# Feed-forward up projections of a two-layer encoder step: eight block products per pair of units replaced by seven

## The chip, the cores and the metric

The kernel runs on one core of a Trainium2 chip. The metric is the device time of one execution in microseconds (us). Before the change the median of 3 runs is 1405.25 us (1405.14 to 1405.56).

## What is computed

One step of a hybrid encoder with 2 layers on 512 prompt tokens and 32 sample tokens, kept side by side as 544 columns; the model width is 1024 and everything is float32. Each layer does

```python
hn = rmsnorm(x)
# retention (4 heads), gated linear attention (4 heads) and band attention (8 heads) from hn @ w_in
x = x + concat([A, B, C]) @ w_out
u = rmsnorm(x) @ w_up                       # 1024 -> 4096
x = x + square(relu(u)) @ w_down            # 4096 -> 1024
```

and a last rmsnorm follows. The change lies in `u`, the up projection, and in what stands around it.

## The kernel before

Activations lie in SBUF as tiles of 128 features by T = 544 tokens; KC = 8 such tiles make the width. A *unit* is a block of 1024 inputs by 128 outputs of a weight matrix, one [128, 1024] tile. A layer has 28 units of input projections, 8 of the output projection (`N_IN + m`) and, in GROUPS = 4 groups, 8 up units and 8 down units each (`N_MLP = 16` a group). So 100 units a layer.

A float32 product is made from two parts of each factor in the type float32r: a *high* part (a copy rounded by ACT) and a *low* part (DVE: the value less its high part). A unit's weights arrive in one of four buffers `raw` (SP, `load`, line 322, which waits until the unit four before it has its low part); ACT writes `whi` (`split`, line 495), DVE `wlo` (`rest`, line 840), in two slots each. PE then runs `products` (line 1376): for each of 8 input tiles high x high, high x low and low x high, each for two halves of HT = 272 tokens, so 48 matmuls of 128x128 weights by 272 columns into two banks of PSUM. Units use two banks of four in turn. Line 1366 records nearly all matmuls.

The feed-forward part: the last output unit's residual is added by DVE (line 1227), ACT makes the scaled high part `xhi` (line 469), DVE the low part `xlo` (line 817), ACT a square that POOL sums up (line 439) for the second norm; POOL then reduces over the partitions (line 445). The norm's factor is applied only to the down projection's result: it is a positive number per token, so it passes through relu and the square as a square, `r2` (lines 1273 and 1278, made once for each group). An up unit's result goes through ACT (relu into `nt`, line 712), DVE (times itself, line 1248), ACT (high part `zhi`, line 715) and DVE (low part `zlo`, line 1251). The down unit 0 waits for these one by one (`ready` in `mlp_unit`, line 1700). A down unit's result is scaled by `r2` on DVE (line 1259) and added to `h` by POOL (line 449). In the last group of a layer `from_down` makes the next layer's first input tiles while the down units run; the last two units of the kernel are done in halves of tokens (`half_products`, line 1390), followed by the final norm.

The order on each engine is written out by hand: `mlp_step(k, g)` of ACT (line 758) and DVE (line 1262) prepares unit k + 1 and finishes unit k - 1. Each engine works its queue in order, so an instruction that waits holds up all that stand behind it. SP's list (line 319 on) has the loads in order of units, with other transfers put between them (`between`, line 389); the state of the gated attention is loaded right after the first load of a layer (`state_in(GLA)`, line 387).

```python
for kc in kcs:                                              # products, line 1379
    for k, (side, act) in enumerate(((whi, hi), (whi, lo), (wlo, hi))):
        for a in range(2):
            ins = mm(PS[:, b + a, 0:HT], side[s][:, w], act[:, kc, a * HT:(a + 1) * HT], ...)
```

Of the kernel before, what the change touches and what calls it, by code (L numbers as in the profile page):

```python
# [20 lines left out]
P = 128  # L21
D = 1024
# [4 lines left out]
L = 2  # L27
# [9 lines left out]
RAW, SPL = 4, 2  # L37
N_IN, N_OUT = 28, KC
N_MLP = 2 * KC
UNITS = N_IN + N_OUT + GROUPS * N_MLP  # L40
PW = 2 * T
# [9 lines left out]


# [63 lines left out]
def f32(ap):  # L116
    return ap.bitcast(F32)


def bank(n):  # L120
# [7 lines left out]
    ss_all=1, newton_act=1, rstd_ready=1, w_in=16 * UNITS // RAW, w_hi=UNITS, w_lo=UNITS, unit_done=UNITS, unit_read=UNITS,  # L128
    pe_low=1, low_read=1, pe_rms=1, pe_z=2, z_act=4, z_min=2, cum_ready=2, r2_steps=3 * GROUPS,
# [8 lines left out]
    relu_ready=GROUPS * KC, z_hi=GROUPS * KC, z_lo=GROUPS * KC, out_dma=16 * 8, stored=96)  # L138
# [14 lines left out]
def hybrid_encoder(nc, x, wu, w_low, a2, small, wf, bias, bias_s, st_ret, st_gla, ck, cv,  # L153
# [3 lines left out]
    with ctx:  # L157
# [81 lines left out]

        PS = ctx.enter_context(nc.psum_tensor("PS", [P, 8, 512], F32))  # L240
# [10 lines left out]
        def sem(name):  # L251
# [25 lines left out]
            "gate_act", "gate_dve", "cat_dve", "cat_hi", "cat_lo", "relu_ready", "z_hi", "z_lo", "out_dma", "stored0", "stored1", "dve_link", "act_link",  # L277
# [8 lines left out]
        def first_piece(eng, n, k):  # L286

            done = piece_in[n][k] if k + 1 < PIECES else sems[f"w_in{n}"]
            cols = slice(k * PIECE, (k + 1) * PIECE)
            eng.dma_start(raw[n][:, cols], wu[n, :, cols]).then_inc(done, 16)  # L290

# [7 lines left out]
        with nc.Block() as block:  # L299
            @block.sync  # L300
            def _(sp):
# [17 lines left out]
                for layer in range(L):  # L319
                    upto = counts(layer)  # L320

                    def load(n):
                        sp.wait_ge(sems["w_lo"], upto("w_lo", n - RAW + 1))
# [3 lines left out]
                    def state_in(kind):  # L327
                        if kind == RET:
# [58 lines left out]
                    state_in(GLA)  # L387

                    between = {10: (rotary_out, 0), 11: (states_out, GLA), 12: (ret_in, 1), 14: (states_out, RET), 15: (band_in, 0),
# [10 lines left out]
                    if layer + 1 < L:  # L400
                        sp.wait_ge(sems["x_lo"], upto("x_lo", 2 * KC))
                        sp.dma_start(sm[:, :], small[layer + 1, :, :]).then_inc(sems["small_in"], 16)
# [15 lines left out]
            def _(pool):  # L418
# [7 lines left out]
                for layer in range(L):  # L426
# [20 lines left out]
                    def add_down(m, g):  # L447
                        pool.wait_ge(sems["unit_read"], upto("unit_read", g * N_MLP + (N_IN + N_OUT + KC + m + 1)))
# [8 lines left out]
            def _(act):  # L457
# [34 lines left out]
                for layer in range(L):  # L492
                    upto = counts(layer)

                    def split(n, g=0):

                        act.wait_ge(sems[f"w_in{n % RAW}"],
                                    upto(f"w_in{n % RAW}", g * (16 * N_MLP // RAW) + 16 * (n // RAW + 1)))
                        if n >= SPL or layer:
# [1358 lines left out]
```

## Time and profile before

| | |
|---|---|
| median of 3 runs | 1405.25 us |
| profiled execution, its own time | 1406.17 us |
| its span in the trace | 1404.2 us |
| busy in the span: PE, DVE, ACT, POOL | 1369.4, 782.6, 531.2, 126.9 us |
| matmuls | 12616, each with its own weight load |
| granted TensorE clock, mean | 0.994 |
| DMA, share of 16 engines | some 30% |

Times in the trace are from the start of the span. Busy time is the time in which an engine has at least one instruction running; matmuls overlap, so the spacing of their starts tells their price, not their duration. A timeline row has the start, the time taken, the engine, the line in the kernel, the operation, what it writes and reads, its shape, how many it merges and, in brackets, the idle time ahead of it with what ended it. A group's row has the count, then the busy time in us and the mean of one in ns, then the idle time before.

### The profile page before, as it was taken

The page shows a single profiled execution, that of the slowest core. Times are in us where ns is not written, and L with a number is a line of the kernel's source. Part 1 is how long each engine was busy: PE and PEld are TensorE (multiplying, and loading weights), DVE is VectorE, ACT ScalarE, POOL GpSimd, SP SyncE. Part 2 cuts the span into 40 slices and gives each one's busy share as a digit, 9 for nine tenths or more (in the row PEclk, how much of TensorE's full clock was granted, in tenths as well). Part 3 has the DMA queues.
Part 4 walks back from the last instruction along what each step waited for, and adds up shares of the span by engine and source line. Part 5 has one row for each costly group of instructions (what it writes and reads, how often), then busy time and mean ns, then how long its engine had stood idle before and what let it go on. Part 6 is the DMA issues. An engine that isn't in the chain of part 4 may idle for free.

```text
span 1404.2 us, 28738 instructions
## 1 busy us (share of the span) xinstructions
PE 1369.4 (98%) x12616; PEld 1331.9 (95%) x12616; DVE 782.6 (56%) x1208; ACT 531.2 (38%) x885; POOL 126.9 (9%) x99
## 2 busy tenths in 40 slices
PE   7999999999999999999999999999999999999997
PEld 7999898899999999999998989889999999999996
DVE  6876767745435335335769676765453353453445
ACT  5333556633213223123333336565332231331333
POOL 0000000031020110210300000001301102002011
PEclk9999999999999999999999999999999999999999
DMA  6133333232222232222221323422222223222221
GB/s 227 61 97 102 95 111 95 77 105 87 86 91 91 91 91 81 87 90 91 93 76 48 99 86 113 144 89 76 91 81 87 90 91 91 91 85 81 91 76 64
DMA packets 56141, 129.78 MB, mean 92 GB/s; under 512 B 11601, under 2 KB 23505, under 8 KB 56017
## 3 DMA queue, kind: packets, MB, share of 16 engines
q1 hardware_dynamic: 55440, 127.42, 29.1%
q8 instruction: 100, 1.64, 0.5%
q10 hardware_dynamic: 576, 0.52, 0.1%
q14 instruction: 25, 0.20, 0.0%
HBM read 118.48 MB, written 7.21 MB: 90 GB/s over the span
## 4 chain that ended last, share of the span: by engine, by line
PE 87%; DVE 7%; ACT 3%; issue 2%; DMA 0%; POOLq 0%; POOL 0%; DVEq 0%; SPq 0%; ACTq 0%
PE PS L1366 85%; PE PS L1605 1%; ACT whi L501 1%; ACT Pr L647 1%; DVE QK L957 1%; DVE Pm L1037 1%; PE PS L1486 1%; DVE F L944 1%; DVE Pr L1140 0%; DVE gb L992 0%; DMA h<-in_x 0%; DVE Pr L1152 0%; ACT ktok L571 0%; DVE O L932 0%; DVE O L1076 0%
## 5 line engine op out<-in xcount | busy, mean ns | idle before, releaser
L843 DVE TENSOR_TENSOR wlo<-raw,whi 128x1024 fp32r<-128x1024 f32 x198 | 248.4, 1254 | 360.1 <-ACT whi L501 359.4
L501 ACT ACTIVATE whi<-raw 128x1024 fp32r<-128x1024 f32 x198 | 209.4, 1058 | 579.6 <-PE PS L1366 579.5
L1366 PE MATMUL PS<-xhi,whi 128*128 128x272 f32 x1920 | 408.1, 294 | 8.0 <-DVE wlo L855 8.0
L1366 PE MATMUL PS<-xhi,wlo 128*128 128x272 f32 x1920 | 399.3, 290 | 0.0
L1366 PE MATMUL PS<-xlo,whi 128*128 128x272 f32 x1920 | 398.3, 289 | 0.0
L1366 PEld LDWEIGHTS PS<-xhi,whi 128*128 128x128 f32 x1920 | 302.6, 189 | 18.7 <-issue 14.5
L1366 PEld LDWEIGHTS PS<-xlo,whi 128*128 128x128 f32 x1920 | 304.0, 190 | 0.0
L1366 PEld LDWEIGHTS PS<-xhi,wlo 128*128 128x128 f32 x1920 | 302.3, 190 | 0.0
L1366 PE MATMUL PS<-zhi,whi 128*128 128x272 f32 x1280 | 267.8, 288 | 0.6 <-DVE wlo L843 0.4
L1366 PE MATMUL PS<-zhi,wlo 128*128 128x272 f32 x1280 | 267.5, 288 | 0.0
L1366 PE MATMUL PS<-zlo,whi 128*128 128x272 f32 x1280 | 266.5, 288 | 0.0
L1366 PEld LDWEIGHTS PS<-zhi,whi 128*128 128x128 f32 x1280 | 202.2, 188 | 1.4 <-DVE wlo L843 0.9
L1366 PEld LDWEIGHTS PS<-zlo,whi 128*128 128x128 f32 x1280 | 202.2, 189 | 0.0
L1366 PEld LDWEIGHTS PS<-zhi,wlo 128*128 128x128 f32 x1280 | 200.8, 189 | 0.0
L449 POOL TENSOR_TENSOR h<-h,sq 128x544 f32<-128x544 f32 x62 | 89.1, 1437 | 650.6 <-DVE sq L1259 650.6
L715 ACT ACTIVATE zhi<-nt 128x544 fp32r<-128x544 f32 x64 | 42.1, 658 | 90.6 <-DVE nt L1248 90.6
L1251 DVE TENSOR_TENSOR zlo<-nt,zhi 128x544 fp32r<-128x544 f32 x64 | 50.0, 781 | 46.4 <-ACT zhi L715 46.4
L1259 DVE TENSOR_TENSOR sq<-PS,r 128x544 f32<-128x544 f32 x62 | 44.6, 719 | 18.5 <-PE PS L1366 18.5
L442 POOL TENSOR_SCALAR ssum<-sq 128x544 f32<-128x544 f32 x2 | 2.4, 1182 | 541.8 <-ACT sq L704 541.8
L647 ACT ACTIVATE Pr<-Pr,mx 128x128 f32<-128x128 f32 (+1 forms) x64 | 35.2, 551 | 34.4 <-DVE mx L1145 34.4
L1248 DVE SCALAR_TENSOR_TENSOR nt<-PS,nt 128x544 f32<-128x544 f32 x64 | 46.0, 719 | 0.0
L712 ACT ACTIVATE nt<-PS 128x544 f32<-128x544 f32 x64 | 38.8, 607 | 0.0
(223 smaller groups left out, 1026.7 us busy)
## 6 DMA issues: line engine op xcount, KB each, us to landing
raw<-in_wu SPq DMA_DIRECT2D x198, 512.0 KB, 3.5
Bh<-in_bias SPq DMA_DIRECT2D x16, 256.0 KB, 4.2
h<-in_x SPq DMA_DIRECT2D x8, 272.0 KB, 5.7
out_k_t<-att_k SPq DMA_DIRECT2D x8, 272.0 KB, 2.2
out_y<-h SPq DMA_DIRECT2D x8, 272.0 KB, 2.3
ckb<-in_ck SPq DMA_DIRECT2D x8, 256.0 KB, 3.5
cvb<-in_cv SPq DMA_DIRECT2D x8, 256.0 KB, 4.8
out_v_p<-vtk SPq DMA_DIRECT2D x8, 256.0 KB, 2.8
```

Of the source, the lines that this page charges most:

```text
L449: nc.gpsimd.tensor_tensor(h[:, m, :], h[:, m, :], sq[m % 2][:, :], ALU.add) \
L501: nc.scalar.activation(whi[n % SPL][:, :], raw[n % RAW][:, :], ACT.Copy).then_inc(sems["w_hi"], 1)
L647: ins = nc.scalar.activation(r, r, ACT.Exp, bias=mx[:, p, i:i + 1], accum_out=rs[:, p, i:i + 1])
L712: nc.scalar.activation(halves(r), PS[:, 2 * (n % 2):2 * (n % 2) + 2, 0:HT], ACT.Relu) \
L715: nc.scalar.activation(zhi[:, k, :], r[:, :], ACT.Copy).then_inc(sems["z_hi"], 1)
L843: nc.vector.tensor_tensor(wlo[n % SPL][:, :], raw[n % RAW][:, :], f32(whi[n % SPL][:, :]), ALU.subtract).then_inc(sems["w_lo"], 1)
L944: ins = nc.vector.tensor_tensor(f.rearrange("p b x h -> p b (x h)"), b.rearrange("p b x h -> p b (x h)"), ref, ALU.subtract)
L957: ins = nc.vector.tensor_tensor(out[:, :, side, :], f[:, :, side, :], blocks(src, c0, c1, H)[:, :, side, :], ALU.mult)
L1248: nc.vector.scalar_tensor_tensor(halves(r), PS[:, 2 * (n % 2):2 * (n % 2) + 2, 0:HT], 0.0, halves(r), ALU.max, ALU.mult).then_inc(sems["un ...
L1251: nc.vector.tensor_tensor(zlo[:, k, :], r[:, :], f32(zhi[:, k, :]), ALU.subtract) \
L1259: nc.vector.tensor_tensor(halves(sq[m % 2]), PS[:, 2 * (n % 2):2 * (n % 2) + 2, 0:HT], halves(r2), ALU.mult).then_inc(sems["unit_read"], 1)
L1366: return nc.tensor.matmul(out, lhsT, rhs, start=start, stop=stop, skip_group_check=True)
```

## The change

Two up units 2j and 2j+1 of a group form a *pair*. With the weights A (unit 2j) and B (unit 2j+1), each cut into inputs 0 to 511 (left) and 512 to 1023 (right), and the activations cut into the same input halves and two halves of 272 tokens, the 2x2x2 block product is formed from seven products of 4 input tiles (Strassen's method in Winograd's form) in place of eight. The weight blocks are `plain` (A as it is), `s12` (two sums), `s4` (half as wide) and `s3` (B with its left half replaced by a difference). They are made on DVE (`pair_sum`, four operations of 512 columns), split into high parts on ACT (`pair_split`) and low parts on DVE (`pair_rest`). There are four slots of `whi` and `wlo` in place of two, the new ones in memory that the attention uses at other times, and the down units use all four.

The activations' combinations `t1`, `tf` are made once per layer while the output projection runs: its units are taken in the order 0, 4, 1, 5, 2, 6, 3, 7, so that tiles of both input halves come in turn. Three products go one after the other into the same bank (P1, P6, P7): ACT copies the running sum out after each (`hold_part`), and PE waits for that copy (`held`) before it adds the next; P5 and P3 share a bank in the same way. DVE's `join` forms the two units' results in `nt` from PSUM and the held sums. Relu, Square and the high part are then three ACT operations on `nt` (`squared_relu`).

Besides: `r2` is made once for each layer, in its first group; the next layer's first two units are split while the last two down units run; the state load `state_in(GLA)` comes four loads later on SP and waits, in the second layer, for the end of the first; twelve matmuls of 128 columns on constants are put at PE's start.

```diff
+WARM = 12
+BLOCKS = ("plain", "s12", "s4", "s3")
+BLOCK_SLOT = dict(plain=2, s12=3, s4=0, s3=1)
+PARTS = dict(P1=("plain", 0, 0), P5=("s12", 0, 1), P2=("plain", 1, 2), P6=("s12", 1, 0), P3=("s4", 0, 1), P7=("s3", 0, 0),
+             P4=("s3", 1, 3))
+OUT_ORDER = (0, 4, 1, 5, 2, 6, 3, 7)
...
 SP
-                    state_in(GLA)
...
+                    between = {5: (state_in, GLA), 10: (rotary_out, 0), 11: (states_out, GLA), 12: (ret_in, 1), 14: (states_out, RET), 15: (band_in, 0),
...
 ACT
+                    def pair_split(q, block):
...
+                        if block == "plain":
+                            weights_in(n, upto)
+                        else:
+                            act.wait_ge(sems["w_sum"], upto("w_sum", 4 * q + (0, 2, 4, 3)[k]))
+                        if j:
+                            act.wait_ge(sems["part_done"], upto("part_done", part_count(q - 1, block)))
...
+                        nc.scalar.activation(whi[slot][:, cols], src[:, cols], ACT.Copy).then_inc(sems["p_hi"], 1)
+                    def hold_part(q, n):
+                        act.wait_ge(sems["part_done"], upto("part_done", 7 * q + PART_NO[("P1", "P5", "P6", "P7")[n]]))
+                        if q:
+                            act.wait_ge(sems["joined"], upto("joined", 4 * (q - 1) + (1, 3, 2, 4)[n]))
+                        else:
+                            act.wait_ge(sems["t_sum"], upto("t_sum", 3 * HK))
+                        nc.scalar.activation(hold[n][:, :], PS[:, pair_bank(q, n == 1), 0:HT], ACT.Copy).then_inc(sems["held"], 1)
+                    def squared_relu(q, r):
+                        k, z = 2 * q + r, nt[r]
+                        act.wait_ge(sems["joined"], upto("joined", 4 * q + 2 * r + 2))
+                        link(nc.scalar.activation(z[:, :], z[:, :], ACT.Relu))
+                        link(nc.scalar.activation(z[:, :], z[:, :], ACT.Square))
+                        nc.scalar.activation(zhi[:, k % KC, :], z[:, :], ACT.Copy).then_inc(sems["z_hi"], 1)
+                    def pair_step(g, j):
+                        q = PAIRS * g + j
+                        if j:
+                            squared_relu(q - 1, 0)
+                        pair_split(q, "s3")
+                        hold_part(q, 0)
+                        if j:
+                            squared_relu(q - 1, 1)
+                        hold_part(q, 1)
+                        if j + 1 < PAIRS:
+                            pair_split(q + 1, "plain")
+                        else:
+                            split_down(g, 0)
+                        hold_part(q, 2)
+                        if j + 1 < PAIRS:
+                            pair_split(q + 1, "s12")
+                            pair_split(q + 1, "s4")
+                        else:
+                            split_down(g, 1)
+                        hold_part(q, 3)
...
 DVE
+                    def new_x(i):
...
+                        nc.vector.scalar_tensor_tensor(tf[:, 1, :], h[:, m, HT:T], by, t1f[:, k, :], ALU.mult, ALU.subtract) \
+                            .then_inc(sems["t_sum"], 1)
+                        dve.wait_ge(sems["t_sum"], upto("t_sum", 3 * k + 1))
+                        nc.vector.tensor_tensor(tf[:, 0, :], tf[:, 1, :], xf[:, k, :], ALU.subtract).then_inc(sems["t_sum"], 1)
+                        nc.vector.scalar_tensor_tensor(tf[:, 2, :], h[:, m, 0:HT], by, tf[:, 1, :], ALU.mult, ALU.subtract) \
+                            .then_inc(sems["t_sum"], 1)
...
+                    def pair_step(g, j):
+                        q, more = PAIRS * g + j, j + 1 < PAIRS
+                        if j:
+                            join(q - 1, 3)
+                        elif g:
+                            scaled(KC - 1, g - 1)
+                        if more:
+                            pair_sum(q + 1, 0)
+                        if j:
+                            z_rest(q - 1, 0)
+                        if more:
+                            pair_sum(q + 1, 1)
+                            pair_sum(q + 1, 2)
+                        pair_rest(q, "s3")
+                        if more:
+                            pair_sum(q + 1, 3)
+                        if j:
+                            z_rest(q - 1, 1)
+                        if more:
+                            pair_rest(q + 1, "plain")
+                        else:
+                            rest_down(g, 0)
+                        join(q, 0)
+                        if more:
+                            pair_rest(q + 1, "s12")
+                        else:
+                            rest_down(g, 1)
+                        join(q, 1)
+                        if more:
+                            pair_rest(q + 1, "s4")
+                        join(q, 2)
...
 PE
+                pe.wait_ge(const_set, 2)
+                for _ in range(WARM):
+                    nc.tensor.matmul(PS[:, 7, 0:P], ones[:, :], ones[:, :], start=True, stop=True, skip_group_check=True)
...
+                    def pair_product(q, name):
+                        block, half, b = PARTS[name]
+                        s, o = BLOCK_SLOT[block], PS[:, pair_bank(q, b), 0:HT]
+                        pe.wait_ge(sems["p_lo"], upto("p_lo", 4 * q + BLOCKS.index(block) + 1))
+                        if name in ("P1", "P5", "P2", "P4"):
+                            bank_free(name, q)
+                        else:
+                            pe.wait_ge(sems["held"], upto("held", 4 * q + dict(P6=1, P3=2, P7=3)[name]))
+                        for i in range(HK):
+                            if q == 0:
+                                operand_ready(name, i)
+                            (hi, lo), w = operand(name, i), slice(half * HD2 + i * P, half * HD2 + (i + 1) * P)
+                            mm(o, whi[s][:, w], hi, name in ("P1", "P5", "P2", "P4") and i == 0, False)
+                            mm(o, whi[s][:, w], lo, False, False)
+                            ins = mm(o, wlo[s][:, w], hi, False, i + 1 == HK)
+                        ins.then_inc(sems["part_done"], 1)
```

## Rows read from the trace of the kernel before

**Rows 1.** The page: busy us, share of the span and instructions of each engine.

```profile
PE 1369.4 (98%) x12616; PEld 1331.9 (95%) x12616; DVE 782.6 (56%) x1208; ACT 531.2 (38%) x885; POOL 126.9 (9%) x99
```

**Rows 2.** The chain that ended last, in order of time: start us, us, what.

```profile
280.31 450.23 PE PS L1366 x3596
...
970.23 403.19 PE PS L1366 x3216
```

**Rows 3.** Windows: us, busy of PE, PEld, DVE, ACT, POOL, clock, DMA share, GB/s.

```profile
20.00:280.00 260.00, 251.89 (x2865) 233.89 (x2863) 187.46 (x378) 127.59 (x262) 0.00 (x0) 0.99 0.31 93
412.70:460.80 48.10, 48.10 (x386) 48.10 (x385) 24.79 (x26) 16.67 (x22) 1.36 (x1) 1.00 0.29 89
```

**Rows 4.** Timeline of PE, 1360 to 1405 us: the first half of unit 6.

```profile
1379.25 0.29 PE L1366 MATMUL PS<-zhi,whi 128*128 128x272 f32 x1
...
1382.15 0.29 PE L1366 MATMUL PS<-zhi,wlo 128*128 128x272 f32 x1
```

**Rows 5.** The page's costliest groups: weights' and activations' high and low parts.

```profile
L843 DVE TENSOR_TENSOR wlo<-raw,whi 128x1024 fp32r<-128x1024 f32 x198 | 248.4, 1254 | 360.1 <-ACT whi L501 359.4
L501 ACT ACTIVATE whi<-raw 128x1024 fp32r<-128x1024 f32 x198 | 209.4, 1058 | 579.6 <-PE PS L1366 579.5
...
L715 ACT ACTIVATE zhi<-nt 128x544 fp32r<-128x544 f32 x64 | 42.1, 658 | 90.6 <-DVE nt L1248 90.6
L1251 DVE TENSOR_TENSOR zlo<-nt,zhi 128x544 fp32r<-128x544 f32 x64 | 50.0, 781 | 46.4 <-ACT zhi L715 46.4
```

**Rows 6.** Operations of 512 and 272 columns: groups by shape, a line's summary, a timeline row.

```profile
L1128 DVE TENSOR_TENSOR Kl<-att_k,Kh 64x512 fp32r<-64x512 f32 x32 | 22.0, 686 | 0.4
...
L663 ACT ACTIVATE PT<-PS 128x512 f32<-128x512 f32 x32 | 17.3, 593 | 1.7 <-PE PS L1605 1.7
...
L781 ACT ACTIVATE nt<-h x4: 430/432/432, 1386.6 to 1394.3; 128x272 f32<-128x272 f32 x4
...
1386.14 0.44 DVE L1304 TENSOR_TENSOR h<-h,sq 128x272 f32<-128x272 f32 x1
```

**Rows 7.** Timeline of DVE: two instructions in a row.

```profile
1362.56 1.23 DVE L843 TENSOR_TENSOR wlo<-raw,whi 128x1024 fp32r<-128x1024 f32 x1 [3.80 <-ACT whi L501]
1363.71 0.71 DVE L1259 TENSOR_TENSOR sq<-PS,r 128x544 f32<-128x544 f32 x1
```

**Rows 8.** DMA issues: count, KB each, median us to landing.

```profile
raw<-in_wu SPq DMA_DIRECT2D x198, 512.0 KB, 3.5
```

**Rows 9.** Timeline of DVE and of ACT after the last output unit of layer 0.

```profile
316.69 0.72 DVE L1227 TENSOR_TENSOR h<-PS,h 128x544 f32<-128x544 f32 x1 [2.94 <-PE PS L1366]
...
317.45 0.75 ACT L469 ACTIVATE xhi<-h,sm 128x544 fp32r<-128x544 f32 x1 [4.47 <-DVE h L1227]
```

**Rows 10.** Timeline of POOL and of DVE, at two places where both work.

```profile
606.14 1.36 POOL L449 TENSOR_TENSOR h<-h,sq 128x544 f32<-128x544 f32 x1 [2.38 <-DVE sq L1259]
...
606.49 2.09 DVE L843 TENSOR_TENSOR wlo<-raw,whi 128x1024 fp32r<-128x1024 f32 x1 [0.43 <-ACT whi L501]
...
325.86 3.43 POOL L445 PARTITION_ALL_REDUCE rstd<-ssum  x1 [5.61 <-issue]
...
326.44 2.38 DVE L1251 TENSOR_TENSOR zlo<-nt,zhi 128x544 fp32r<-128x544 f32 x1 [0.72 <-ACT zhi L715]
```

**Rows 11.** Timeline at the start: PE's first matmuls.

```profile
7.97 0.79 PE L1366 MATMUL PS<-xhi,whi 128*128 128x272 f32 x2 [7.97 <-DVE wlo L855]
...
8.56 0.66 PE L1366 MATMUL PS<-xlo,whi 128*128 128x272 f32 x2
...
11.28 0.66 PE L1366 MATMUL PS<-xlo,whi 128*128 128x272 f32 x2
```

**Rows 12.** Timeline of DVE near the end: the last unit's weights and the scaling behind them.

```profile
1380.60 1.23 DVE L843 TENSOR_TENSOR wlo<-raw,whi 128x1024 fp32r<-128x1024 f32 x1 [3.52 <-ACT whi L501]
1381.74 0.72 DVE L1259 TENSOR_TENSOR sq<-PS,r 128x544 f32<-128x544 f32 x1
```

More of the change, by code:

```diff
@@ L523, in _ @@
                     else:
-                        split(1)
                         from_down(KC - 1, layer)
@@ L755, in _ @@
                             new_x(m - 1)
[L756 to L768 removed]
+                            t_high(m - 1)
@@ new lines, in down_step @@
+                    def down_step(g, m):
+                        if m == 0:
+                            for r in range(2):
+                                squared_relu(PAIRS * g + PAIRS - 1, r)
+                        for n in DOWN_AHEAD[g].get(m, ()):
+                            split_down(g, n)
+                        if g + 1 < GROUPS:
+                            for k, block in ((5, "plain"), (6, "s12"), (7, "s4")):
+                                if m == k:
+                                    pair_split(PAIRS * (g + 1), block)
+                        else:
+                            if layer + 1 < L and m >= 6:
+                                split_next(m - 6)
+                            if m >= 2:
+                                from_down(m - 2, layer + 1)
@@ new lines, in down_step @@
+                    def down_step(g, m):
+                        if m == 0:
+                            q = PAIRS * g + PAIRS - 1
+                            join(q, 3)
+                            z_rest(q, 0)
+                            z_rest(q, 1)
+                        for n in DOWN_AHEAD[g].get(m, ()):
+                            rest_down(g, n)
+                        if m and (not final(layer, g) or m + 1 < KC):
+                            scaled(m - 1, g)
+                        if m == 0 and g == 0:
@@ new lines, in down_unit @@
+                    def down_unit(g, m):
+                        def ready(kc):
+                            pe.wait_ge(sems["z_lo"], upto("z_lo", g * KC + (kc + 1)))
+                        begin_down(g, m)
+                        products(N_IN + m, (zhi, zlo), all_kc, ready=None if m else ready, slot=down_slot(g, m))
+                    for g in range(GROUPS):
+                        for j in range(PAIRS):
+                            for name in PARTS:
+                                pair_product(PAIRS * g + j, name)
+                        for m in range(KC - 2 if final(layer, g) else KC):
+                            down_unit(g, m)
@@ L1759, in weight_units @@
         out += [unit(w_in[l][:, c]) for c in cols]
-        out += [unit(w_out[l][:, m * P:(m + 1) * P]) for m in range(KC)]
+        out += [unit(w_out[l][:, m * P:(m + 1) * P]) for m in OUT_ORDER]
         for g in range(GROUPS):
```

396 lines of the change are left out of this document (293 added, 103 removed).

## The prediction

> **What bounds the kernel now.** I read the page's busy shares first: PE is busy 98% of the span, DVE 56%, ACT 38% [rows 1], so work taken from PE shortens the run as long as nothing else has to wait. The chain of waits shows where PE is the limit without a break: one piece from 280.31 us runs 450.23 us over 3596 matmuls, another from 970.23 us runs 403.19 us over 3216 [rows 2]. Those are the output projection and the feed-forward part of each layer, and they give 450.23/3596 = 0.1252 and 403.19/3216 = 0.1254 us for a matmul of 272 columns. The windows then show how much room the other engines have in one up stage (eight units, 48.10 us): PE 48.10 busy, DVE 24.79, ACT 16.67 [rows 3]. A pair of up units takes 96 matmuls, 12.03 us, and in it DVE works some 6.2 us and ACT 4.2.
>
> **What is removed.** A pair of up units becomes seven products of 4 input tiles x 3 (high by high, high by low, low by high) = 84 matmuls in place of 96. There are 2 layers x 4 groups x 4 pairs = 32 pairs, so 32 x 12 = 384 matmuls go. The new products work on one half of the tokens at a time, so that a loaded weight tile serves one half only; the kernel's last two units already run so, and there 24 matmuls start from 1379.25 to 1382.15 us, 2.90/23 = 0.126 us apart [rows 4]. So the price is the same: 384 x 0.1253 = 48.1 us off PE's path. [...]
>
> **What is added in an up step.** In the time of one pair (84 x 0.1253 = 10.53 us) DVE now has three low parts of 1024 columns at 1.254 and two of 544 at 0.781 [rows 5], one low part and four sums of 512 columns, of which the trace has no exact like (64x512 took 0.686 [rows 6], a sum of 128x512 has the same columns: 0.69), and four joins of 272 columns at 0.44 [rows 6]: 3.76 + 1.56 + 0.69 + 2.76 + 1.76 = 10.5 us. That is PE's 10.53 exactly, and before it was half. But a DVE instruction that waits for nothing starts 1.15 us after one of 1.23 us [rows 7], 0.08 less than the duration; with 14 instructions the bill is between 9.4 us (all overlap) and 10.5 + 14 gaps of 0.04 = 11.1 us (none does). I take 9.4 to 9.8, since most of them have their inputs long before. ACT has three copies of 1024 columns (1.058) and one of 512 (0.593), four holds (0.43) and two times Relu, Square, Copy (0.66 each) [rows 5, 6]: 3.77 + 1.72 + 3.96 = 9.4 us.
>
> Both fit, so the question is the order. I walk one step, time 0 at the start of P1, the products ending at 1.5, 3.0 ... 10.5 and readable 0.2 later (a matmul lasts 0.29 for a spacing of 0.125). ACT: first unit of the pair before finished 1.1, split of the s3 block 2.1, P1 held 2.5, second unit 4.4, P5 held 4.8, next plain block (free after P2) 5.8, P6 held 6.6, s12 7.6, s4 (free after P3) 8.3, P7 held 9.6. DVE: last join of the pair before 0.6, sum 1.2, low part of the first unit 1.9, two sums 3.0, s3 4.2, sum 4.8, low part of the second unit 5.4, plain 7.0, join 7.4, s12 8.9, join 9.3, s4 9.9, third join 10.3. Against that, P6 starts at 4.5 and needs P1 held (2.5); P3 at 6.0 needs P5 held (4.8); P7 at 7.5 needs P6 held (6.6) and s3 (4.2); the next P1 needs plain at 10.5 (7.0), the next P5 s12 at 12.0 (8.9). All are early, the least by 0.9 us, and the step ends as it began, so it repeats. Loads: a pair's second raw buffer is free only with s3, 4.2 into the step; its load takes 3.5 us [rows 8] and is wanted one step later at 11.1. The down units keep 48 matmuls each; two units of prepared weights lie ahead in place of one, worth nothing, since PE did not wait there. At the turn to the down units the last pair's low part comes at 3.8 us against 5.3 for the matmul that reads it. The reciprocals go from 16 to 4, hidden. The state load that is moved behind four weight loads on SP is first read many units later, and its wait for the layer before is over by then.
>
> **The turn from output projection to the first pair, once in each layer.** Today PE goes on at once: after the last unit there come only the residual (0.72 at 316.69), the high part (0.75 at 317.45) [rows 9] and the low part, under 42 matmuls that don't need them. Now the last tile also needs three differences of 272 columns, a high copy of 816 and its low part. From the residual's start on (PE stopped 0.2 before): high part 1.5, low part 2.3, differences 3.5, ACT's copy of 816 (between 0.59 and 1.06) 4.4, DVE's low part 5.5; and behind that copy in ACT's queue stand s3 (5.4) and the hold of P1 (5.8), which P6 wants at 4.3: 1.5 us of idle PE. POOL can make this longer. At 606.49 a DVE subtraction that met a POOL addition took 2.09 us where 1.23 is usual, ending 1.1 after POOL did; under the 3.43 us reduction at 325.86 one took 2.38 where 0.78 is the mean [rows 5, 10]. One such hold of 1.36 puts the idle at 2.8 us, the reduction's 1.6 may add 0.3. So 1.5 to 3.1 us per layer; I take 2.3, twice: 4.6 us.
>
> **Start and end.** Twelve matmuls are put ahead of the first loads' arrival. The first real ones go at half pace, 12 of them from 8.56 to 11.28 us, 0.227 each, which is 272 columns at 1.2 GHz [rows 11]; there are some 16 such, so at most 16 x 0.102 = 1.6 us can be won, and nothing if the some 4 us between the extra matmuls and the first product undo them. They cost nothing, as PE idles until 7.97 [rows 11]. Between 0 and 1.6 no row decides; I take 0.8. At the end DVE need not do the last weights (1.23 at 1380.60) before the scaling at 1381.74 [rows 12]: the work after it comes up to 1 us earlier on a chain that has other waits; 0 to 1, I take 0.5.
>
> **Sum.** -48.1 + 4.6 - 0.8 - 0.5 = -44.8 us. The profiled execution took 1406.17 us for a span of 1404.2, 0.9 above the median of 1405.25: 1406.17 - 44.8 = 1361.4, and against the median **1360.5 us**.
>
> **Rivals.** *DVE sets the step.* If DVE's instructions don't overlap, a step lasts 11.1 us and more with POOL's addition in the first step of a group (1.36). For it: the bill of 10.5 is PE's time. Against: overlap of 0.08 is seen wherever inputs are ready. Price: 0.6 x 3 steps x 8 groups = 14 us, so 1375. *The hand-overs run in series.* ACT and DVE wait for each other around a loop: join, first unit, s3, hold, second unit, hold, plain, hold, s12 on ACT, s12 on DVE, join; in my walk that is 9.5 us. From 10.53 on it takes from the gain, at 12.03 plus what the turns cost nothing is left: 1405. For it: a queue in which one late instruction delays all behind it; against: it needs 2.5 us in every step that no row shows. *The clock falls.* The new waits of P6, P3 and P7 for holds leave PE idle in short pieces in each pair, and if TensorE drops to its lower level, a matmul takes 0.227 in place of 0.125: 84 x 0.102 = 8.5 us a pair. From the sixth pair of 32 on the kernel is slower than before; with half of the pairs it is 1360 + 16 x 8.5 = 1496 us. Against it: from 20 to 280 us PE idles 8.1 us in many short pieces, and its granted clock there is 0.99 [rows 3], the upper level. [...] That the arithmetic is not what it says is no rival: seven products of 12 matmuls can be counted in the change.
>
> **Chances.** Forecast 0.66; DVE sets the step 0.25; series of hand-overs 0.05; clock 0.04. About 0.2% (2.8 us) is what a measurement of this kernel can tell from no change. The first two are faster; the third is split between the same (0.03) and slower (0.02), the fourth is slower. Faster 0.91, same 0.03, slower 0.06. The range starts where the turns cost nothing and start and end give all (-48.1 - 1.6 - 1.0, 1354.5) and reaches over the second case: 1354.5 to 1376. The forecast's own range is 1355 to 1365.
>
> **What would show it.** Right: 84 matmuls a pair at 0.125, some 10.53 us from P1 to P1; PE idle only at the two turns, 1.5 to 3 us each, put down to ACT's hold or DVE's t parts; DVE some 90% busy in up stages. Wrong: PE waiting in every pair for a hold, or for a low part with DVE never idle (second case); a spacing of 0.227 in up stages (clock); first products still at 0.227 would mean that the extra matmuls give nothing.

## The result and the profile after

The changed kernel takes **1372.74 us** (median of 4 runs, 1371.65 to 1373.25) against 1405.4 for the kernel before, in the same comparison: a ratio of 0.9767, 95% interval 0.975 to 0.9783. So 32.7 us are won where 44.8 were forecast: the time lies in the range given, but 12 us above the forecast and 7.7 above the forecast's own range. The profiled execution took 1371.65 us, 34.5 less than the one before.

The page's busy shares after the change, to be read beside [rows 1]:

```profile
PE 1330.8 (97%) x12256; PEld 1291.3 (94%) x12256; DVE 968.1 (71%) x1494; ACT 677.6 (49%) x1165; POOL 136.6 (10%) x99
```

384 products are gone and 24 records of the twelve new ones came, hence 12256. The chain that ended last has two long pieces of matmuls again, which answer to [rows 2]:

```profile
338.97 373.57 PE PS L1697 x2984
...
998.61 355.34 PE PS L1697 x2814
```

373.57/2984 = 0.1252 us a matmul: the price is the old one. But in the kernel before the piece of layer 0 began at 280.31, in the output projection; now it begins at 338.97, in the second pair of up units. The windows of the stretch between show why (busy PE, PEld, DVE, ACT, POOL, then the granted clock):

```profile
278.31:302.00 23.69, 23.69 (x189) 23.69 (x190) 21.85 (x28) 12.08 (x20) 7.59 (x5) 1.00 0.34 109
320.00:338.97 18.97, 14.88 (x106) 14.50 (x104) 17.74 (x23) 11.22 (x19) 5.21 (x2) 0.91 0.17 56
338.97:700.00 361.03, 361.03 (x2892) 359.51 (x2893) 241.67 (x290) 174.96 (x258) 54.31 (x37) 1.00 0.30 94
...
412.70:454.80 42.10, 42.10 (x338) 42.10 (x337) 34.91 (x49) 31.51 (x51) 1.74 (x1) 1.00 0.32 101
```

Everything after the turn is PE without a break, the up steps (last row, four pairs in 42.1 us) included. The place that answers to 280.31 is now 278.31. From there to 338.97 lie 420 matmuls (of the 3596 before, 192 are gone and 2984 follow): 288 of the output projection, 84 of the first pair and 48 of the second. 420 x 0.1252 = 52.6 us, and they take 60.66. **Layer 0 loses 8.1 us at this turn** and layer 1 loses 8.4 (the like stretch, 952.16 to 1013.16), at places that the timeline of PE names:

```profile
314.24 0.42 PE L1697 MATMUL PS<-zhi,wlo 128*128 128x272 f32 x2
314.49 0.29 PE L1697 MATMUL PS<-xhi,whi 128*128 128x272 f32 x1
...
317.33 0.39 PE L1697 MATMUL PS<-xhi,whi 128*128 128x272 f32 x1 [1.17 <-DVE wlo L1061]
...
318.92 0.39 PE L1697 MATMUL PS<-xhi,whi 128*128 128x272 f32 x1 [0.19 <-DVE xlo L1501]
...
324.76 0.55 PE L1697 MATMUL PS<-th,whi 128*128 128x272 f32 x1 [3.69 <-issue]
325.10 0.43 PE L1697 MATMUL PS<-tl,whi 128*128 128x272 f32 x1
...
328.05 0.36 PE L1697 MATMUL PS<-xhi,wlo 128*128 128x272 f32 x1
...
338.97 0.36 PE L1697 MATMUL PS<-xhi,whi 128*128 128x272 f32 x1 [0.40 <-ACT hold L623]
```

The output projection's last product starts at 314.24 and P1 follows at once. P5 waits 1.17 for its weights and, ahead of its fourth and last input tile, 0.19 for the low part of `t1`; P2 follows without a wait, and P6 waits 3.69, the large one. Behind it 15 matmuls run 0.227 us apart (the granted clock from 324.76 to 328.25 is 0.51) before the spacing is 0.125 again. That costs 15 x 0.102 = 1.5 us on top of the waits, and P3 of the second pair waits 0.40 more for a hold. Layer 1 has the same three waits (1.18, 0.19, 3.69) and 24 matmuls at half pace, 2.4 us (granted clock 0.51 from 998.61 to 1004.15).

The wait of P6 is marked "issue", but P6 waits for P1's hold, and PE goes on at 324.76, as the first of ACT's two holds from 324.29 ends. Why that hold is late has to be read on the other engines. DVE around it:

```profile
306.62 1.60 DVE L1489 SCALAR_TENSOR_TENSOR tf<-h,sm,t1f 128x272 f32<-128x272 f32 x1
...
311.00 1.23 DVE L1061 TENSOR_TENSOR wlo<-raw,whi 128x1024 fp32r<-128x1024 f32 x1 [1.90 <-ACT whi L614]
...
316.05 1.83 DVE L1061 TENSOR_TENSOR wlo<-s,whi 128x1024 fp32r<-128x1024 f32 x2 [1.45 <-ACT whi L614]
317.80 0.71 DVE L1469 TENSOR_TENSOR h<-PS,h 128x544 f32<-128x544 f32 x1
...
320.03 1.60 DVE L1489 SCALAR_TENSOR_TENSOR tf<-h,sm,t1f 128x272 f32<-128x272 f32 x1
...
327.46 2.88 DVE L1051 TENSOR_TENSOR s<-raw,s 128x512 f32<-128x512 f32 x1
```

and ACT:

```profile
309.14 0.89 ACT L852 ACTIVATE th<-tf 128x816 fp32r<-128x816 f32 x1 [3.28 <-DVE tf L1493]
309.93 1.04 ACT L614 ACTIVATE whi<-raw 128x1024 fp32r<-128x1024 f32 x1
...
314.98 1.56 ACT L614 ACTIVATE whi<-s 128x1024 fp32r<-128x1024 f32 x2
...
322.55 0.88 ACT L852 ACTIVATE th<-tf 128x816 fp32r<-128x816 f32 x1 [2.71 <-DVE tf L1493]
323.34 1.04 ACT L614 ACTIVATE whi<-raw 128x1024 fp32r<-128x1024 f32 x1
324.29 0.67 ACT L623 ACTIVATE hold<-PS 128x272 f32<-128x272 f32 x2
```

and POOL:

```profile
305.93 1.99 POOL L516 TENSOR_TENSOR ssum<-ssum,sq 128x544 f32<-128x544 f32 x1 [4.88 <-ACT sq L842]
...
319.92 1.41 POOL L516 TENSOR_TENSOR ssum<-ssum,sq 128x544 f32<-128x544 f32 x1 [4.09 <-ACT sq L842]
326.95 3.88 POOL L522 PARTITION_ALL_REDUCE rstd<-ssum  x1 [5.63 <-issue]
```

Two things make the wait. **A loop of queues:** ACT copies the plain block of the first pair (309.93) only behind a tile's t parts, for which it waited 3.28 us on DVE; DVE then waits 1.90 for that copy (311.00) and 1.45 for the next (316.05), and the last residual, whose matmuls were over at 314.66, comes only at 317.80, because DVE had the first pair's s12 and s4 ahead of it. **Meetings with POOL:** where POOL adds squares, a DVE difference of 272 columns takes 1.60 us and ends 0.3 after POOL's addition (306.62 beside 305.93, 320.03 beside 319.92); and DVE's sum at 327.46 takes 2.88 beside the all-reduce. In the rows of the additions POOL starts first and DVE ends last (additions end at 307.92 and 321.33, differences at 308.22 and 321.63); beside the all-reduce DVE's sum also starts second, but it ends 0.5 us before the all-reduce's recorded end (330.34 and 330.83).

### The profile page after: what moved, and what is told of

The parts are those of the page before. It is cut to its first block, busy times and chain, and to the rows that moved or that the text cites. A ratio compares the mean times of both kernels' runs of the same rounds, so it can differ in the third digit from the quotient of the medians.

```text
span 1369.5 us, 29045 instructions
## 1 busy us (share of the span) xinstructions
PE 1330.8 (97%) x12256; PEld 1291.3 (94%) x12256; DVE 968.1 (71%) x1494; ACT 677.6 (49%) x1165; POOL 136.6 (10%) x99
## 4 chain that ended last, share of the span: by engine, by line
PE 82%; DVE 11%; ACT 3%; issue 2%; DMA 0%; DVEq 0%; SPq 0%; ACTq 0%
PE PS L1697 80%; PE PS L1946 1%; DVE wlo L1061 1%; ACT Pr L776 1%; ACT whi L579 1%; DVE QK L1199 1%; DVE Pm L1279 1%; PE PS L1827 1%; DVE F L1186 1%; DVE Pr L1382 0%; DVE xlo L990 0%; DVE h L1469 0%; ACT whi L614 0%; DVE gb L1234 0%; DVE ssum L1000 0%
## 5 line engine op out<-in xcount | busy, mean ns | idle before, releaser
L1697 PE MATMUL PS<-xhi,whi 128*128 128x272 f32 x1408 | 343.7, 296 | 3.4 <-DVE wlo L1061 2.4
L1697 PE MATMUL PS<-xlo,whi 128*128 128x272 f32 x1408 | 334.3, 289 | 0.0
L1697 PE MATMUL PS<-xhi,wlo 128*128 128x272 f32 x1408 | 333.5, 289 | 0.0
L1697 PEld LDWEIGHTS PS<-xhi,whi 128*128 128x128 f32 x1408 | 238.1, 190 | 15.5 <-issue 7.2
L1697 PEld LDWEIGHTS PS<-xlo,whi 128*128 128x128 f32 x1408 | 238.8, 190 | 0.0
L1697 PEld LDWEIGHTS PS<-xhi,wlo 128*128 128x128 f32 x1408 | 237.9, 190 | 0.0
L1029 DVE TENSOR_TENSOR wlo<-raw,whi 128x1024 fp32r<-128x1024 f32 x64 | 97.4, 1530 | 35.5 <-ACT whi L596 35.4
L1697 PE MATMUL PS<-th,whi 128*128 128x272 f32 x384 | 112.4, 293 | 7.4 <-issue 7.4
L1697 PE MATMUL PS<-th,wlo 128*128 128x272 f32 x384 | 112.3, 292 | 0.0
L1697 PE MATMUL PS<-tl,whi 128*128 128x272 f32 x384 | 111.6, 291 | 0.0
L1061 DVE TENSOR_TENSOR wlo<-raw,whi 128x1024 fp32r<-128x1024 f32 x64 | 78.0, 1219 | 12.6 <-ACT whi L614 12.5
```

The costliest lines, as they stand in the source:

```text
L1029: nc.vector.tensor_tensor(wlo[slot][:, :], raw[n % RAW][:, :], f32(whi[slot][:, :]), ALU.subtract) \
L1061: nc.vector.tensor_tensor(wlo[slot][:, cols], src[:, cols], f32(whi[slot][:, cols]), ALU.subtract) \
L1697: return nc.tensor.matmul(out, lhsT, rhs, start=start, stop=stop, skip_group_check=True)
```

## The experiments

Each kernel is the changed one with the edit named, of which the core is shown; its time stands against 1372.74.

**Short additions on POOL.** The squares of seven of the eight tiles are summed on 32 columns instead of 544, so most of the second norm's sum is left out.

```diff
-nc.gpsimd.tensor_tensor(ssum[:, :], ssum[:, :], sq[m % 2][:, :], ALU.add)
+nc.gpsimd.tensor_tensor(ssum[:, 0:32], ssum[:, 0:32], sq[m % 2][:, 0:32], ALU.add)
```

> Seven of POOL's eight additions of squares per layer work on 32 columns in place of 544; the second norm's sum is left out for the other columns. Theory (the turn from the output projection to the first pair is late because DVE meets POOL's additions: t1f and tf operations of 272 columns took 1.60 us where 0.50 is usual, at 299.76, 306.62 and 320.03 us): these fall to 0.5, DVE comes 2 to 3 us earlier to the last unit's residual, and of the 8.1 us lost per layer 3 to 4.5 come back; the whole run 6 to 9 us shorter, 1364 to 1367. Rival (the hand-written order on ACT and DVE makes the turn long, whatever POOL does): under 2 us of 1372.7 in all.

Measured: 1366.44 us (1365.8 to 1367.43; ratio to before 0.9714, 0.9697 to 0.9731), 6.3 less. The same DVE instructions in this kernel's timeline:

```profile
305.93 0.49 DVE L1489 SCALAR_TENSOR_TENSOR tf<-h,sm,t1f 128x272 f32<-128x272 f32 x1
...
318.24 0.50 DVE L1489 SCALAR_TENSOR_TENSOR tf<-h,sm,t1f 128x272 f32<-128x272 f32 x1
```

They took 1.60 before. Both waits of P5 are gone, that of P6 is 2.42 us, and in layer 0 no matmul behind it is at half pace. The sum that meets the all-reduce still takes 2.87. So the meetings with the additions are worth 3.2 us a layer, with what they drag along in waits and in the clock, and they are not the whole loss.

**The first hold ahead of the last t parts.** P1's running sum is copied to spare memory before ACT's last copy of 816 columns, so that it waits neither for the t sums nor for s3.

```diff
                     new_x(KC - 1)
+                    hold_part(0, 0)
                     t_high(KC - 1)
```

> ACT copies P1's sum out before the high part of the last tile's differences, into a spare tile of memory, so that the copy no longer stands behind it and behind the s3 block. Theory (P6's wait of 3.69 us at 324.76 is this hold in ACT's queue): P6 starts right after P2 at 320.9, stops at its fourth input tile until the low part at 324.5, and the pair is then limited by s3's low part at 327.5 in place of 329.4 for P7: 1.5 to 3 us per layer, 3 to 6 us in all, and the stretch at 1.2 GHz after the wait gets shorter. Rival (P6's wait is set by the late differences themselves, the hold being only the name in the record): the wait moves to the fourth tile and under 1.5 us in all is won.

Measured: 1371.85 us (1370.95 to 1373.25; 0.9753, 0.9735 to 0.977), 0.9 less, which is within the runs' spread. P6 now waits for the low part of the t sums in place of the hold:

```profile
323.60 0.59 PE L1699 MATMUL PS<-th,whi 128*128 128x272 f32 x1 [2.34 <-DVE tl L1508]
```

The wait fell from 3.69 to 2.34, but it is the lateness of the t sums that sets the step: the hold was only the last in line.

**No matmuls ahead of the loads.** `WARM = 0` in place of 12.

> The twelve matmuls ahead of the first products are taken away, all else stays. Theory (they are what makes the first products start at 0.125 us spacing, and they also keep a stretch near 60 us at the upper clock level): 1.9 to 3.5 us longer than 1372.7, first products at 0.227. Rival (the first products are earlier because the loads came earlier in that execution): within 0.7 us of 1372.7.

Measured: 1374.82 us (1373.97 to 1376.36; 0.9775, 0.9754 to 0.9796), 2.1 more. PE's timeline at the start, without the twelve:

```profile
7.65 0.79 PE L1697 MATMUL PS<-xhi,whi 128*128 128x272 f32 x2 [7.65 <-DVE wlo L1098]
8.24 0.66 PE L1697 MATMUL PS<-xlo,whi 128*128 128x272 f32 x2
8.69 0.66 PE L1697 MATMUL PS<-xhi,wlo 128*128 128x272 f32 x2
```

The same view of the changed kernel, with them:

```profile
1.12 5.49 PE L1682 MATMUL PS<-ones 128*128 128x128 f32 x24 [1.12 <-POOL ones L497]
6.91 0.69 PE L1697 MATMUL PS<-xhi,whi 128*128 128x272 f32 x2 [0.31 <-DVE wlo L1098]
7.44 0.41 PE L1697 MATMUL PS<-xlo,whi 128*128 128x272 f32 x2
```

Two products lie 0.45 us apart without them (0.227 each), 0.25 with them. The granted clock reads 1.00 in both (8.24 to 11.86 and 7.44 to 12 us), so the record shows two paces at the start and not two clocks. Each of the twelve float32 products is recorded as two, and together they last until 6.61, so PE idles only 0.31 us before its first real product. Not all of the 2.1 us need be theirs: the first product starts 0.74 us later here, and 0.59 of that is the first transfer of the input, which took 4.23 us in this execution and 3.64 in the other. From 50 to 60 us the granted clock is 0.83 without them and 1.00 with them; but the kernel with the reordered turn (below) has them too and shows 0.83, so that this stretch stays fast because of them is not shown.

**More work on DVE in each step.** Three, and in another kernel one, additions of 512 columns in each of the 24 steps that prepare a further pair, results unused.

```diff
                             pair_sum(q + 1, 2)
+                            for _ in range(3):
+                                a = raw[raw_no(g, 2 * j + 2) % RAW][:, 0:HD2].rearrange("p (x c) -> p x c", x=2)
+                                nc.vector.tensor_tensor((t1f[:, 0:2, 0:256], t1f[:, 2:4, 0:256], tf[:, 0:2, 0:256])[_], a, a, ALU.add)
```

> Three more DVE additions of 512 columns (0.6 us each from start to start) in each of the 24 up steps that prepare a next pair; their results are used by nothing. Theory (a step is bound by PE, DVE has some 1.3 us of idle time in it, and the order has 0.9 us of margin): a step gets longer by 1.8 less 0.9 to 1.3, so by 0.5 to 0.9, 12 to 22 us in all. Rival (DVE already bounds the steps): 24 x 1.8 = 43 us.

Measured: 1383.09 us (1381.43 to 1386.16; 0.9834, 0.9812 to 0.9857), 10.4 more, 0.43 a step.

> The whole computation, and one more DVE addition of 512 columns (about 0.6 us, result unused) in each of the 24 steps. The run with three cost 0.43 us a step of some 1.8 us added, so the margin of DVE in a step is about 1.4 us and one addition of 0.6 us fits into it: 0 to 2 us over the changed kernel, 1372 to 1375 us. Rival, DVE sets the step: 14 us more, 1387 us.

Measured with one: 1373.55 us (1372.26 to 1374.29; 0.9772, 0.9755 to 0.979), 0.8 more, which is within the runs' spread. So 0.6 us more of DVE in a step cost next to nothing, and of 1.8 some 1.4 were hidden: that is DVE's margin, and PE sets the step.

**The all-reduce later.** POOL's all-reduce alone waits for the third pair's second tile.

```diff
                     pool.wait_ge(sems["sq_used"], upto("sq_used", KC))
+                    pool.wait_ge(sems["joined"], upto("joined", 4 * 2 + 2))
                     nc.gpsimd.partition_all_reduce(rstd[:, :], ssum[:, :], P, RADD).then_inc(sems["ss_all"], 1)
```

> The whole computation; POOL's all-reduce alone waits for the third pair's second tile, nothing else is moved. The trace of the changed kernel has it at 326.95 us, behind the idle of 3.69 us, and DVE's low part beside it takes 2.88 us. Theory, it stands behind the stall and costs only the 0.57 us that follow in the first step: 0 to 1.5 us less over both layers, 1371.2 to 1372.7 us. Rival, its lock is a large part of the turn: 2.2 us per layer less, 1368 us.

Measured: 1372.56 us (1371.88 to 1373.15; 0.9765, 0.9749 to 0.978), no change.

**PE kept busy in its wait.** Fourteen products of ones by ones ahead of the first pair's P6, into P4's bank.

```diff
+                            if q == 0 and name == "P6":
+                                for _ in range(14):
+                                    mm(PS[:, pair_bank(0, 3), 0:P], ones[:, :], ones[:, :])
                             pe.wait_ge(sems["held"], ...)
```

> The whole computation; in each layer PE does 14 products of ones by ones (128 columns, result unused, into the bank that P4 overwrites later) where it waits 3.69 us ahead of the first pair's P6; nothing else is moved. In the start of the changed kernel 12 such products took 5.49 us at the lower clock, so 14 take 3.2 us at the higher one and fit into the wait. Theory, the half pace of the 15 and 22 matmuls behind the wait (0.227 us each and not 0.125) is the price of PE having been idle, so 1.5 and 2.2 us come back: 1369 us (1368.5 to 1370.5). Rival, the pace has another cause (the weights, the blocks that DVE and ACT still split): 1372 to 1374 us.

Measured: 1373.58 us (1371.82 to 1373.64; 0.9769, 0.9753 to 0.9785), no change, though PE's timeline shows that the edit did what it should:

```profile
320.22 3.29 PE L1697 MATMUL PS<-ones 128*128 128x128 f32 x28
324.02 0.39 PE L1697 MATMUL PS<-th,whi 128*128 128x272 f32 x1 [0.52 <-ACT hold L623]
324.25 0.29 PE L1697 MATMUL PS<-tl,whi 128*128 128x272 f32 x1
324.38 0.29 PE L1697 MATMUL PS<-th,wlo 128*128 128x272 f32 x1
...
330.82 0.39 PE L1697 MATMUL PS<-xhi,whi 128*128 128x272 f32 x1 [0.50 <-DVE wlo L1061]
```

The 14 products take 3.29 us, 0.235 each, where the 12 at the start took 0.458 each; the granted clock reads 1.00 in both stretches (320.22 to 324.02 here, 1.12 to 6.61 in the changed kernel), and that the start ran at a lower clock was the author's estimate from its pace. The matmuls behind the wait start 0.125 us apart and not 0.227, and the granted clock from 324.02 to 328 us is 1.00, so the half pace of this place does come from PE's idling, and this expectation held for the pace but not for the time. The time won ends in front of DVE: the next pair's low part is late (330.82), because the all-reduce (3.91 us from 326.22) held a sum here as it did at 327.46 above:

```profile
326.76 2.87 DVE L1051 TENSOR_TENSOR s<-raw,s 128x512 f32<-128x512 f32 x1
```

**Both together.** The last two edits in one kernel.

> The whole computation; the 14 filling products in PE's wait ahead of P6 and the later all-reduce together, which alone gave nothing each (1373.58 and 1372.56 us). Theory, each hid the other: with the filling PE keeps 0.125 us a matmul but then waits 0.50 us for a low part that the all-reduce made late and some 0.9 us for holds; with the later all-reduce DVE is early but PE runs at 0.227 us. Together 1 to 2 us per layer come back: 1368.5 to 1370.7 us. Rival, neither is on the path (the holds or the blocks behind DVE's late start set the first step whatever these two do): 1372 to 1374 us.

Measured: 1368.94 us (1367.49 to 1371.4; 0.9743, 0.9729 to 0.9756), 3.8 less. The half pace of PE and the meeting of DVE with the all-reduce had hidden each other: either alone measures as nothing, both together as 1.9 us a layer.

**The order of the turn.** ACT takes the plain block ahead of the eighth output unit's weights, s12 and s4 ahead of the t parts of the sixth and the seventh unit, and at the end the last tile's high part, s3, the hold (in spare memory), the t parts and the square in this order; DVE follows; and the all-reduce waits as above. So four things change together: the order on ACT and DVE, the place of the hold, that of the last square, and the all-reduce. The core of it on ACT:

```diff
+                        if m == 6:
+                            pair_split(0, "plain")
                         if m + 1 < KC:
                             split(N_IN + m + 1)
...
                             new_x(m - 1)
+                            if m == 6:
+                                pair_split(0, "s12")
+                            if m == 7:
+                                pair_split(0, "s4")
                             t_high(m - 1)
-                        if m == 6:
-                            pair_split(0, "plain")
-                        if m == 7:
-                            pair_split(0, "s12")
-                            pair_split(0, "s4")
-                    new_x(KC - 1)
+                    act.wait_ge(sems["unit_read"], upto("unit_read", N_IN + KC))
+                    xhi_tile(KC - 1, KC)
+                    pair_split(0, "s3")
+                    hold_part(0, 0)
                     t_high(KC - 1)
...
```

> The whole computation, with the order of the turn changed: ACT splits the first pair's plain block, S1+S2 and S4 each ahead of work of the last tiles, DVE takes their low parts so too and S3's between the last tile's xlo and its t parts; the first product is held ahead of ACT's last t_high, in spare memory; POOL's all-reduce waits for the third pair's second tile. If the 8.1 us that each layer loses at the turn come from DVE and ACT reaching the last tile late because the first pair's splits stand in front of them in the wrong order, then 4 to 6 us per layer come back: 1361 to 1365 us. Rival, the meetings with POOL set the turn by themselves: no more than the 6.3 us of the run with short additions and, with these additions still whole, rather 0 to 2 us: 1371 to 1373 us.

Measured: **1361.03 us** (1360.07 to 1361.61; 0.968, 0.9663 to 0.9698), 11.7 less. P5 does not wait any more, and P6 waits 1.27:

```profile
322.05 0.39 PE L1707 MATMUL PS<-th,whi 128*128 128x272 f32 x1 [1.27 <-DVE tl L1514]
...
334.33 0.36 PE L1707 MATMUL PS<-xhi,whi 128*128 128x272 f32 x1 [0.47 <-ACT hold L624]
```

Its chain has the same 2984 matmuls in one piece, 4.64 us earlier than at 338.97:

```profile
334.33 373.59 PE PS L1707 x2984
```

The meetings with POOL's additions are still there, on other instructions, as in this row of DVE (0.78 us is its usual time):

```profile
307.52 1.88 DVE L1486 SCALAR_TENSOR_TENSOR xlo<-h,sm,xhi 128x544 fp32r<-128x544 f32 x1
```

So the 11.7 us were not won by avoiding them. How they divide among the four changes was not tried; the hold alone gave 0.9 and the all-reduce alone 0.2, both within the spread, but two changes at this place need not add up, as the run before showed.

**The order and the short additions together**, the sum of the second norm again left out for the most part.

> The changed order of the turn and POOL's additions on 32 columns together; it leaves out the rest of the second norm's sum, so its output is not the reference's. Theory, the meetings with POOL and the order of ACT and DVE are together the whole loss of the turn: 0.5 to 1.5 us per layer are left of 8.1, so 13 to 15 us less than the changed kernel, 1357.5 to 1359.5 us. Rival, the two are one loss told twice: what the better of the two gives alone, 1361 to 1366 us.

Measured: 1358.58 us (1356.76 to 1359.16; 0.9663, 0.9648 to 0.9678), 2.5 less than with the order alone, and the two waits of 1.27 are gone. So of the 14.2 us that both edits give, the meetings account for 6.3 if they go first and for 2.5 if the order goes first. This fits a cost that comes for the most part through the queues that they make late; that it does is argued and not shown.

**The squares later.** With the order changed, ACT takes the last three tiles' squares at the ends of the first three pairs' steps, so that POOL's additions and the all-reduce lie there, complete.

```diff
                         hold_part(q, 3)
+                        if q < 3:
+                            square(5 + q)
```

> The whole computation; the order of the turn as in the run with the changed order, and the squares of the last three tiles taken by ACT at the ends of the first three pairs' steps, so that POOL's three additions and its all-reduce lie in the steps. Theory, POOL's meetings with DVE at the turn are the 2.5 us that the run with changed order and short additions gained over the changed order alone, and in a step they fit into DVE's margin of 1.4 us: 1358.5 to 1359.5 us. Rival, a meeting in a step costs there what it cost at the turn: 1361 us or more.

Measured: 1360.42 us (1360.25 to 1361.12; 0.9681, 0.9666 to 0.9695), between the two theories and not to be told from the order alone. P6 has no wait left, but the meeting with the all-reduce now lies in the last step before the down units, as DVE's timeline shows:

```profile
354.96 2.93 DVE L1041 TENSOR_TENSOR wlo<-raw,whi 128x1024 fp32r<-128x1024 f32 x1
```

and PE waits once more in each layer, in the down units:

```profile
370.62 0.49 PE L1711 MATMUL PS<-zhi,whi 128*128 128x272 f32 x2 [0.50 <-DVE sq L1554]
```

A low part of 1.22 us took 2.93 beside the all-reduce (3.67 us from 354.19); whether the wait of 0.50 comes from that was not tried. This and the kernel with the order alone are the fastest whole ones.

## Why the prediction was right, and where it was off

**What is removed: right.** 384 matmuls fewer at 0.1252 each: 48.1 us, and loading a weight tile for one half of the tokens costs nothing that the trace shows: the 336 matmuls of the four pairs from 412.70 to 454.80 are 0.1253 apart, and 0.1252 was the price before.

**The up step: right.** DVE's order in a step that has a pair before it and one behind it was walked in advance. The second step of the second group is one; its P1 starts at 423.24:

```profile
426.24 1.22 DVE L1061 TENSOR_TENSOR wlo<-raw,whi 128x1024 fp32r<-128x1024 f32 x1
...
429.10 1.22 DVE L1061 TENSOR_TENSOR wlo<-raw,whi 128x1024 fp32r<-128x1024 f32 x1 [0.41 <-ACT whi L614]
...
430.83 1.22 DVE L1061 TENSOR_TENSOR wlo<-s,whi 128x1024 fp32r<-128x1024 f32 x1 [0.16 <-ACT whi L614]
...
432.93 0.43 DVE L1077 TENSOR_TENSOR nt<-hold,hold 128x272 f32<-128x272 f32 x1
```

s3 is through at 4.2 (walked: 4.2), plain at 7.1 (7.0), s12 at 8.8 (8.9), the third join at 10.1 (10.3). The window of this step:

```profile
423.20:433.72 10.52, 10.52 (x86) 10.52 (x85) 9.35 (x14) 8.65 (x15) 0.00 (x0) 1.00 0.31 102
```

DVE is busy 9.35 of 10.52 us, 89%, as expected: the bill of 10.5 with all overlaps, 9.4. Over the four steps it is 34.91 of 42.10 us, 83%, because the last step prepares no pair and has 6.72.

**The rivals.** "DVE sets the step" would have given 1375 us, close to the 1372.74 measured, but for another reason: its loss lies in every step, and PE has none there; one more addition of 0.6 us would have cost 14 us and cost 0.8. The hand-overs do not run in series either. The clock falls (to 0.51), but once in a layer, behind a wait of 3.69 us, and not in the pairs (1.00 from 338.97 to 700 us). The reading against this rival was too quick, though: the 0.99 of the window from 20 to 280 us is a mean, and inside it the kernel before has a fall, behind one wait of 1.91 us:

```profile
51.52 1.14 PE L1366 MATMUL PS<-QK 64*64 64x32 f32 x64 [1.91 <-DVE Pm L1009]
...
53.41 0.66 PE L1366 MATMUL PS<-xhi,wlo 128*128 128x272 f32 x2
53.86 0.66 PE L1366 MATMUL PS<-xhi,whi 128*128 128x272 f32 x2
```

Two matmuls are 0.45 apart there, and the granted clock from 54 to 56 us is 0.50. So the trace held a case of what a wait can cost beyond its own length.

**The turn: the term that failed.** The step "From the residual's start on (PE stopped 0.2 before)" with its "I take 2.3, twice: 4.6 us" measured 8.1 and 8.4: 16.5. Its chain from the residual on was sound: high part 1.5, low part 2.3, t sums 3.5, hold 5.8 were walked, and from 317.80 the rows give 1.5, 2.3, 4.7 and about 6.9, the 1.1 more being the meeting that the text bounded. What was wrong is the bracket: the residual does not start 0.2 us after PE but 3.1 after its last matmul (314.66 and 317.80), because DVE stands in its queue in front of the first pair's blocks, whose copies ACT has behind the t parts of the tile before. I had walked the up step over both queues and the turn over one. Nor had the term a price for the clock: 1.5 and 2.4 us of the loss are the half pace behind P6's wait. With the queues in the other order the turn loses 2.9 us (420 matmuls from 278.77 to 334.33, 55.56 us against 52.6) and the time is 1361.03 us, beside a forecast of 1360.5. That the order of the queues at the turn, with the three smaller changes made along with it, is the cause is so shown; its share against the meetings depends on which goes first.

**Start: off by up to 1.3.** 0.8 was taken between 0 and 1.6, because some 4 us might lie between the extra matmuls and the first product. There are 0.31: 2.1 us by the run without them, of which some 0.6 may be the earlier input; the share of the twelve stays open. The 1.2 GHz of the prediction and of the expectation on the first hold is 272 columns divided by 0.227 us and no clock that was read: the granted clock from 8.56 to 11.74 us is 1.00 in the kernel before. **End:** the last scalings come 34.7 us earlier in the profile; with the terms above, -48.1 + 16.5 - 2.0 (278.31 in place of 280.31) leaves 1.1 for the end and all else, where 0.5 was taken. What was to show the turn right, 1.5 to 3 us of idle PE put down to ACT's hold or DVE's t parts, showed it wrong: 3.69 alone ahead of P6, and 1.36 more ahead of P5 and inside it, which no step had named.

**What was luck.** The forecast's own range, 1355 to 1365 us, was missed. The wider one holds 1372.74 only because it was stretched over the case in which DVE sets the step, and that case did not happen.

## What to carry to other kernels

Where one stage passes into the next, walk every engine's queue through the hand-over, not only the chain of the data: an instruction that feeds the stage after next can stand in front of the one that PE wants now, as the first pair's s12 and s4 did here, which put the last residual 3.1 us behind its matmuls. Two losses at one place can hide each other, so that removing either shows nothing; before a suspect is dropped, remove it together with its neighbour (1373.58 and 1372.56 us alone, 1368.94 together, against 1372.74). Matmuls on constants in the wait kept the pace behind it at 0.125 us here, with a granted clock of 1.00, but this paid only when the work behind the wait was ready for the faster pace.

## What the runs showed of the hardware

**The clock behind a wait.** In the changed kernel, waits of 3.69 us with nothing on PE were followed by 15 matmuls at 0.227 us in layer 0 and 24 in layer 1, each time with a granted clock of 0.51. A wait of 2.42 us in the kernel with short additions was followed by none in layer 0 (1.00 from 321.88 to 325 us), one of 2.45 in layer 1 by some 15 (0.52 from 993.59 to 997.12), which began only after four at the full pace. One of 2.34 in the kernel with the earlier hold was followed by 13 in layer 0 (0.51 from 323.60 to 326.66). The wait of 1.91 us was followed by half pace in the kernel before (51.52; 0.50 from 54 to 56), and in the changed kernel, at the same place (49.62), by a granted clock of 1.00. Behind the waits of 1.27 us in the reordered kernel it stayed at 1.00 too (322.05 to 330 and 980 to 1005 us). So in these runs the length of a wait alone does not tell what follows. With the wait filled by 28 records on constants the pace stayed at 0.125 and the clock at 1.00. At the start the pace of 0.227 stands beside a granted clock of 1.00 (kernel before, 8.56 to 11.74 us; kernel without the twelve matmuls, 8.24 to 11.86).

**DVE under a POOL addition.** In these rows a DVE instruction that starts while a POOL addition runs ends behind the addition's recorded end by most of its own usual time: 0.29 to 0.31 us for one of 0.5 (272 columns, all twelve beside additions of squares in the changed kernel), 0.58 for one of 0.78 (544 columns, 307.52 in the reordered kernel, where the addition ran from 306.39 to 308.82), and 1.1 for one of 1.23 (1024 columns, [rows 10]). Whether every kind of DVE instruction is held so is not shown. An all-reduce of 3.88 us held one of 0.68 us for 2.88, though not up to its recorded end.
